# Openings of each sub-layer rebuilt around a normalised copy of x, with the order of attention, index and weight splitting changed

## The reference

```
h = rmsnorm(x, g_pre) * (1.0 + scale) + shift
x = x + resid_w * gate * rmsnorm(y_fn(h), g_post)
```

## Time and profile before

| what | value |
|---|---|
| median of 3 runs | 2760.48 us (2760.14 to 2760.69) |
| the profiled execution | 2764.69 us, span of its instructions 2761.9 us |
| TensorE busy | 2717.2 us, 98% of the span |
| VectorE busy | 1518.2 us, 55% |
| ScalarE busy | 1096.0 us, 40% |
| GpSimd busy | 269.6 us, 10% |
| granted TensorE clock, mean | 0.995 of full speed |

### The profile page before, as it was taken

How to read it: one execution, slowest core, us unless ns; L and a number is a source line. 1 busy time by engine, 2 the same in 40 slices (tenths; PEclk the granted TensorE clock), 3 DMA queues, 4 the chain that set the end, 5 groups by cost and what they waited for, 6 DMA issues and landing times.

```text
span 2761.9 us, 37653 instructions
## 1 busy us (share of the span) xinstructions
PE 2717.2 (98%) x13280; PEld 2177.1 (79%) x13280; DVE 1518.2 (55%) x2565; ACT 1096.0 (40%) x1993; POOL 269.6 (10%) x353
## 2 busy tenths in 40 slices
PE   8999999999999999999999999999999999999999
PEld 6888887676777888888888888866677778888887
DVE  6665455567746656532376553554677475553323
ACT  4322234665545343222242222446655453332221
POOL 0111000122100001110011100001221000011100
PEclk9999999999999999999999999999999999999999
DMA  8554522112222416523245545222122224152332
GB/s 301 209 203 158 160 94 86 61 54 62 70 86 75 115 54 229 182 99 107 84 157 194 197 159 153 88 77 62 54 67 70 87 75 116 68 183 91 99 107 69
DMA packets 94797, 321.85 MB, mean 117 GB/s; under 512 B 16769, under 2 KB 17153, under 8 KB 93378
## 3 DMA queue, kind: packets, MB, share of 16 engines
q1 hardware_dynamic: 94658, 320.07, 35.3%
HBM read 316.72 MB, written 2.13 MB: 115 GB/s over the span
## 4 chain that ended last, share of the span: by engine, by line
PE 87%; DVE 6%; ACT 3%; issue 2%; DVEq 1%; SPq 0%; DMA 0%; POOL 0%; ACTq 0%; POOLq 0%
PE bank L485 20%; PE bank L487 20%; PE bank L486 20%; PE bank L494 7%; PE bank L492 7%; PE bank L493 7%; PE bank L1852 2%; PE bank L1872 2%; ACT w_high L463 1%; DVE w_low L469 1%; PE bank L1843 1%; DVEq L1059 1%; PE bank L1816 1%; DVE scores_sb L1241 1%; PE bank L1738 1%
## 5 line engine op out<-in xcount | busy, mean ns | idle before, releaser
L485 PE MATMUL bank<-h_high,w_high 128*128 128x512 f32 (+1 forms) x2488 | 970.0, 390 | 13.7 <-DVE h_low L1358 11.2
L487 PE MATMUL bank<-h_high,w_low 128*128 128x512 f32 (+1 forms) x2488 | 948.7, 381 | 0.0
L486 PE MATMUL bank<-h_low,w_high 128*128 128x512 f32 (+1 forms) x2488 | 947.5, 381 | 0.0
L469 DVE TENSOR_TENSOR w_low<-w_raw,w_high 128x1024 fp32r<-128x1024 f32 x438 | 566.3, 1294 | 595.4 <-ACT w_high L463 593.8
L463 ACT ACTIVATE w_high<-w_raw 128x1024 fp32r<-128x1024 f32 x438 | 459.2, 1051 | 362.1 <-PE bank L494 319.0
L485 PEld LDWEIGHTS bank<-h_high,w_high 128*128 128x128 f32 x2488 | 472.5, 190 | 112.0 <-issue 24.5
L487 PEld LDWEIGHTS bank<-h_high,w_low 128*128 128x128 f32 x2488 | 471.0, 189 | 91.2
L486 PEld LDWEIGHTS bank<-h_low,w_high 128*128 128x128 f32 x2488 | 472.0, 190 | 84.0 <-issue 1.9
L492 PE MATMUL bank<-w_high,ffn_high 128*128 128x512 f32 x704 | 273.9, 389 | 0.0
L493 PE MATMUL bank<-w_high,ffn_low 128*128 128x512 f32 x704 | 273.9, 389 | 0.0
L494 PE MATMUL bank<-w_low,ffn_high 128*128 128x512 f32 x704 | 273.9, 389 | 0.0
(11 more groups left out here) (216 smaller groups left out, 2638.2 us busy)
## 6 DMA issues: line engine op xcount, KB each, us to landing
w_raw<-stream SPq DMA_DIRECT2D x438, 512.0 KB, 3.6
ada_raw<-ada SPq DMA_DIRECT2D x128, 512.0 KB, 3.6
ada_start<-ada SPq DMA_DIRECT2D x8, 1024.0 KB, 17.8
post_gain<-post_gain_row SPq DMA_DIRECT2D x6, 512.0 KB, 6.0
mixer_consts<-mixc SPq DMA_DIRECT2D x2, 1152.0 KB, 5.3
x<-x_in SPq DMA_DIRECT2D x4, 512.0 KB, 6.6
silu_c<-silu_row SPq DMA_DIRECT2D x4, 512.0 KB, 4.2
out<-x SPq DMA_DIRECT2D x8, 256.0 KB, 2.0
```

Of the source, the lines that this page charges most:

```text
L469: eng.tensor_tensor(wL[:, slot], raw[:, slot], wH[:, slot].bitcast(F32), ALU.subtract).then_inc(lo_ready[slot].sem, 1)
L485: eng.matmul(o, a, rhs_h, start=first, stop=False)
L486: eng.matmul(o, a, rhs_l, start=False, stop=False)
L487: return eng.matmul(o, b, rhs_h, start=False, stop=last)
```

## The change

1. x_norm: instead of building a diagonal, ACT writes x times its per-token factor into a new tile `x_norm` (in the space of h_low), one activation of 128 x 1024 for each token block; blocks 0, 1 and 2 inside the closing, block 3 in the opening. POOL's L662 goes. PE transposes x_norm plainly with the identity (`pe.transpose`, one instruction instead of two for each 128 x 128).
2. Of the 8 feature tiles of a pair, 2, 3, 6 and 7 are scaled and shifted on ACT (`full` in ACT's opening, into `h_full_act`), the others on DVE; h_high stays on ACT, h_low on DVE. A hand-written order replaces the loops.
3. DVE takes h_full of tiles 0 and 1 of the first pair, and their h_low, ahead of block 3's update of x; ACT takes block 3's squares after tiles 0 to 3.
4. Branch C's scores move from the end of every fourth step to its head.
5. `("qrope", 1)` moves from before `("wi",)` to after the eighth index step.
6. In DVE's list the `split_low` that belongs to a unit done in quarters is kept back until after the next attention step's work (or the next unit).

```diff
             yield ("att", st)
-            if st == 0:
-                yield ("scores", st)
...
-            if 0 < st < STEPS and st % 4 == 0:
-                yield ("scores", st)
...
-                ("qrope", 0), ("uq", 1), ("ukv",), ("qrope", 1), ("wi",)]
+                ("qrope", 0), ("uq", 1), ("ukv",), ("wi",)]
...
         yield ("index", n // HEADS + 1, n % HEADS)
         if n % 3 == 2:
             yield fill.pop(0)
+        if n == HEADS - 1:
+            yield ("qrope", 1)
...
+            def x_norm(l, n, tb):
+
+                s.wait_ge(rsx_ready.sem, rsx_ready.at(l, TB * n + tb + 1))
+                s.activation(xn[:, :, tb * P:(tb + 1) * P], x[:, tb].rearrange("p (k n) -> p k n", k=KD), ACT.Copy,
+                             scale=rsx[:, tb:tb + 1]).then_inc(xn_ready.sem, 1)
+
             def closing(l, n, u_last):
...
+                    if tb >= 1:
+                        x_norm(l, n, tb - 1)
                     if tb == 2:
                         split_high(s, l, u_last + 1)
...
+                    if tb < TB - 1:
+                        x_squares(l, n, tb)
...
+                high(0, 0)
+                high(0, 1)
+                full(0, 2)
+                high(0, 2)
+                full(0, 3)
+                high(0, 3)
+                x_squares(l, n, TB - 1)
+                full(0, 6)
+                high(0, 4)
+                high(0, 5)
+                x_norm(l, n, TB - 1)
+                high(0, 6)
+                full(0, 7)
+                high(0, 7)
+                split_high(s, l, u_first + LEAD)
...
-                if kind in UNIT_KINDS and it != MIXER[0] and (kind != "out" or it[1] < KD - LEAD):
+                if kind in UNIT_KINDS and kept is not None:
+                    split_low(v, l, kept)
+                    kept = None
+                if it in PARTED:
+                    kept = U_OF[it] + LEAD
+                elif kind in UNIT_KINDS and it != MIXER[0] and (kind != "out" or it[1] < KD - LEAD):
                     split_low(v, l, U_OF[it] + LEAD)
...
                     vector_attention(v, l, it[1])
+                    if kept is not None:
+
+                        split_low(v, l, kept)
+                        kept = None
...
+                mean_y(l, n, TB - 1)
+                full(0, 0)
+                full(0, 1)
+                scaled_y(TB - 1)
+                low(0, 0)
+                low(0, 1)
+                v.drain()
+                update_x(l, n, TB - 1)
+                v.drain()
+                full(0, 4)
+                low(0, 2)
+                full(0, 5)
+                low(0, 3)
+                mean_x(l, n, TB - 1)
+                for j in range(4, KD):
+                    low(0, j)
...
             def h_block(tb):
-                pe.wait_ge(diag_ready.sem, diag_ready.at(l, TB * n + tb + 1))
+                pe.wait_ge(xn_ready.sem, xn_ready.at(l, TB * n + tb + 1))
...
-                    mm = pe.matmul(bank[4 + j // 2][:, at:at + P], x[:, tb, j * P:(j + 1) * P], diag[:, tb],
-                                   start=True, stop=True)
+                    mm = pe.transpose(bank[4 + j // 2][:, at:at + P], xn[:, j, tb * P:(tb + 1) * P], ident[:, :])
...
-                if br != "C" and g % 2 == 0:
+                if br == "C" and g % 4 == 0:
+
+                    if g > 0:
+                        pe.wait_ge(shifted.sem, shifted.at(l, g))
```

More of the change, by code:

```diff
@@ L671, in closing @@
                     if not ends(l, n):
[L672 removed]
+                        rstd(l, n, tb)
             def reciprocals(l, g):
@@ L937, in opening, with full, high @@
             def opening(l, n, u_first):
[L939 to L945, removed]
+                shift = shift_col(n % NB)
+                def full(pair, j):
+                    s.wait_ge(tr_ready.sem, tr_ready.at(l, KD * (n + 1) + 4 * pair + j // 2 + 1))
+                    if j >= 6:
+                        s.wait_ge(h_ready.sem, h_ready.at(l, h_at(n) + KD * pair + j - 3))
+                    s.activation(hu_act[:, j % 2], bank[4 + j // 2][:, 2 * P * (j % 2):2 * P * (j % 2 + 1)],
+                                 ACT.Identity, scale=vecA[:, j:j + 1], bias=shift(j)).then_inc(hua_ready.sem, 1)
+                def high(pair, j):
+                    done = KD // 2 * (2 * (n + 1) + pair) + 2 * (j // 4) + j % 2 + 1
+                    if j % 4 < 2:
+                        s.wait_ge(hu_ready.sem, hu_ready.at(l, done))
+                        src = hu[:, j % 2]
+                    else:
+                        s.wait_ge(hua_ready.sem, hua_ready.at(l, done))
+                        src = hu_act[:, j % 2]
+                    s.activation(hH[:, j, 2 * P * pair:2 * P * (pair + 1)], src, ACT.Copy).then_inc(hh_ready.sem, 1)
+                high(0, 0)
[13 more added lines that the diff above has]
+                split_high(s, l, u_first + LEAD)
+                full(1, 2)
+                high(1, 0)
+                high(1, 1)
+                full(1, 3)
+                high(1, 2)
+                high(1, 3)
+                full(1, 6)
+                high(1, 4)
+                high(1, 5)
+                full(1, 7)
+                high(1, 6)
+                high(1, 7)
             def shift_col(which):
@@ L1323, in mean_x, with mean_y, scaled_y, update_x @@
                                        ).then_inc(msx_ready.sem, 1)
-            def closing(l, n, u_last):
[L1327 to L1332, removed]
+            def mean_y(l, n, tb):
+                c = slice(tb, tb + 1)
+                v.wait_ge(ssq1_ready.sem, ssq1_ready.at(l, TB * n + tb + 1))
+                v.scalar_tensor_tensor(msy[:, c], ssq1[:, c], 1.0 / D, ssq0e[:, c], ALU.mult, ALU.add
+                                       ).then_inc(msy_ready.sem, 1)
+            def scaled_y(tb):
+                v.tensor_tensor(yg1[:, :], bank[tb][:, :], gain[:, T:D], ALU.mult)
+            def update_x(l, n, tb):
+                c = slice(tb, tb + 1)
+                v.wait_ge(rsy_ready.sem, rsy_ready.at(l, TB * n + tb + 1))
+                for half, y in ((0, yg0[:, tb]), (1, yg1[:, :])):
+                    xt = x[:, tb, T * half:T * half + T]
+                    v.scalar_tensor_tensor(xt, y, rsy[:, c], xt, ALU.mult, ALU.add).then_inc(x_ready.sem, 1)
+            def closing(l, n, u_last):
+                for tb in range(TB if ends(l, n) else TB - 1):
+                    mean_y(l, n, tb)
+                    scaled_y(tb)
                     v.drain()
[L1334 to L1337, removed]
+                    update_x(l, n, tb)
                     if ends(l, n):
@@ L1352, in opening, with low @@
                 shift = shift_col(n % NB)
-                def low(i):
-                    pair, j = i // KD, i % KD
+                def low(pair, j):
                     cols = slice(2 * P * pair, 2 * P * (pair + 1))
[L1357 to L1367, removed]
+                    v.wait_ge(hh_ready.sem, hh_ready.at(l, h_at(n) + KD * pair + j + 1))
+                    v.tensor_tensor(hL[:, j, cols], (hu if j % 4 < 2 else hu_act)[:, j % 2],
+                                    hH[:, j, cols].bitcast(F32), ALU.subtract).then_inc(h_ready.sem, 1)
@@ L1376, in opening @@
+                split_low(v, l, u_first + LEAD)
+                v.drain()
+                full(1, 0)
+                full(1, 1)
+                low(1, 0)
+                low(1, 1)
+                v.drain()
+                full(1, 4)
+                low(1, 2)
+                full(1, 5)
+                for j in range(3, KD):
+                    low(1, j)
                 v.drain()
```

65 lines of the change are left out of this document (28 added, 37 removed).

## The result

The kernel after takes 2726.84 us, the median of 4 runs (2724.39 to 2729.41), beside 2760.59 (2760.14 to 2764.03) of the kernel before on the same chip: ratio 0.9875, 95% interval 0.9858 to 0.9892, which lies wholly under 1. That is 33.7 us less; the forecast had 24.3 less, and its range ended at 2727.0, 0.16 us above the measured median. The direction was right, the size too small by 9.4 us.

The account below looks back on a forecast made before the run. PE, busy for 98% of the span, was taken to bound the kernel; openings 11.0, qrope 7.3 and attention 6 sum to 24.3 us, taking the profiled 2764.7 to 2740.4, the median 4.2 lower: 2736.2 us, range 2727 to 2748.

Parts of the forecast that it names:

- I take half of the waits: 6 us: Attention, both layers: half of the 11.2 us of PE's waits taken as gain, 6 us saved.
- The bound at the good end, 14: Attention at best: all 11.2 us of waits and two half-rate stretches of 1.46 go, 14 us saved.
- The bound at the bad end: Attention at worst: 14 groups of scores wait about 1.1 us each, less 7.2 now waited at transposes: 8 lost.
- signs: Attention: waits less than half of 11.2 us, none over 0.5 at C heads; wrong if near 1 us in branch C.
- Openings: Five openings, first transpose to first 512-column product: 25.3 us each after the change, 11.0 us saved in all.
- at most 0.6: Openings: a half-rate stretch at the first products slows PE where it would idle anyway, costing at most 0.6 us.
- qrope: Index steps: moving the second rotation removes the waits for `wi` and the half-rate stretches behind them, 7.3 us saved.
- The clock falls a second time in each opening: Openings: clock falls again behind the second pair of transposes, slowing products by 7.3 us in all; 2743.5 us, chance 0.20.
- Attention gives nothing: Attention: waits only move from the transposes to the head of the scores; 18.3 us saved, 2742.2 us, chance 0.18.
- Openings give nothing: Openings: x_norm(3) delays h_block(2) by 3 us instead of 0.9, an opening takes 27.4; 2747 us, chance 0.08.
- Slower: Attention: PE stalls for `shifted` at 14 group heads and the clock falls after each, 36 us; 2778 us, chance 0.03.
- Better than all this: Both bounds at their good end, 14 us for attention and 9 for qrope; 2727 us, chance 0.04.

Follow-up runs that it names:

- e2: Kernel before with both attention edits alone: branch C's scores at the head of every fourth step and the weight splits kept back; 2750.78 us, ratio 0.9954.
- e4: Kernel before with only the weight splits kept back behind the attention step, scores where they were; 2765.3 us, ratio 1.0007.
- e5: Kernel before with only branch C's scores moved to the head of the step, weight splits as they were; 2753.85 us, ratio 0.9966.
- e9: Kernel after without the kept back split, the C scores still at the head of the step; 2734.54 us, ratio 0.9895.
- e6: Kernel after with all 32 transposes of each opening as two-instruction multiplications by the identity; 2736.28 us, ratio 0.9905.
- e1: Kernel before with only the second rotation of the queries moved behind the eighth index step; 2757.82 us, ratio 0.9979.
- e3: Kernel before with only the openings changed (points 1 to 3 of the change); 2745.46 us, ratio 0.9934.
- e10: Kernel after with two-instruction transposes in the first two blocks of each opening, plain ones in the last two; 2726.69 us, ratio 0.9866.
- e12: Kernel after with two-instruction first-pair transposes, tile 6's rounding ahead of x_norm(3) on ACT and a weight split moved forward; 2725.45 us, ratio 0.9860.

## Why the prediction was too small

**The step that failed: attention, "I take half of the waits: 6 us".** 12.6 us in the trace, 12.4 measured alone (e2). Half of the 11.2 us of listed waits is 5.6, and as a guess at idle time that was right: 5.4 less in the two layers, 4.3 of it in the list. The step was wrong to take the waits for the whole. It left nearly nothing for the two half-rate stretches behind the wait in D, about 3 us, which are gone, and nothing for the 4.2 us by which PE's busy time over the same instructions fell besides, and which are in no wait. That the bound at the good end, 14, lies so near is therefore luck: it had all 11.2 us of waits going. The bound at the bad end was wrong too: the stall at the head of the C scores is 1.0 once in each layer (L1916), where it had 1.1 fourteen times. And one wait is indeed turned into another for each edit alone (e4: all of it, e5: about half of the 12.6), but much less for the two together (e2, e9). The forecast named signs: waits under half of the 11.2, none over 0.5 at the heads of C, and as a sign of being wrong waits near 1 us there. All three went against it (6.9 left, 1.0 in each layer), and attention still gave twice the term.

**Openings: the order of the terms right, two sizes off.** 11.0 forecast, 15.7 in the traces. The sum had 25.3 for an opening: 4.65 to the first product, 8.1 to h_block(2), 12.6 for the rest. Measured without a half-rate stretch 4.24, 7.42 and 12.60, together 24.26. DVE is free at 392.3 and not at 392.6, as x_norm(1) fits into ACT's idle time but for 0.17 us (its next w_high starts at 386.59 instead of 386.42). Between the first product and h_block(2) I had waits of 0.7 and 0.9; there is 0.94 in all. So 1.0 too much in each, 5 in all, less 0.4 for the third opening, whose first wait is longer. The two stretches cost 1.1 where 0.9 was allowed for all. Five times 25.3 is also 126.5 and not 126.3. The transposes were nearly exact: 0.11 apart, 1.69 to 1.72 for a pair against 1.76, and the old ones 3.59 (e6) against 3.75, so that the second pair saves 1.9 and not 2.0. That a half-rate stretch would cost "at most 0.6" now was right (24.84), though it came in two openings and not in most.

**qrope: right in the traces.** 7.3 forecast, 7.7 in the trace of the whole, 7.2 in that of e1, whose median gives 5.4. The wait for `wi` is gone with the stretch behind it.

**Not in the sum.** 3.2 us of the traces' difference are the half-rate stretch in the mixer's first products of layer 1, of which the new openings may have a part, as said above. The profiled execution of before (2764.7) stood at the top of its runs, that of after (2724.39) at the bottom, so the medians differ by less than the traces.

**The rivals.** *The clock falls a second time in each opening*: no stretch begins behind the second pair in any opening of any trace, 0 of 40 with plain transposes there and 0 of 30 with two instructions. The rule of the Trainium skill, TensorE: Matmul & The Clock Gate, Part 4, would have had plain transposes leave the clock low; here they run 0.109 us apart at a granted clock of 1.00 and 0.213 at 0.50 (e5), so they do run at the full clock. Whether they count less for keeping it isn't settled: the 15 of 25 against 10 of 25 above leave room for that. *Attention gives nothing*: refuted by e2. *Openings give nothing*: refuted by e3; x_norm(3) delays h_block(2) by 0.9 at most and not by 3. *Slower*, PE stalling at 14 heads: e5 shows its mechanism at two groups in each layer, for 1.0 to 1.1; it needed 1.3 at all fourteen. *Better than all this* at 2727 was the nearest, but not for its reasons: it had 14 for attention by way of the waits and 9 for qrope, and the openings' 15.7 weren't in it.

**What stays open.** Why the mixer's first products, where PE waits for nothing, draw a half-rate stretch in some traces and not in others (none in after, one in each layer in e10 and e12), and in every trace with the old openings, is open. It is worth 1.6 us each time.

## What to carry to other kernels

When two edits aim at the same chain of waits, price them together: each alone was worth 0 and 8.7 us here, both together 12.4. Nor are listed waits the whole price: 4.3 us of them went, and attention got 12.6 shorter. Read idle time from the spacing of PE's starts or from its busy time over a fixed set of instructions, not from the list of waits alone. And where an engine must open a new stage, put the first two tiles of it ahead of the closing work that nobody needs yet: that one change of order was worth as much as halving the transposes.

## What was not expected of the hardware

The first pair of transposes can be twice as long at nearly no cost. Transposes of 3.73 us with a wait of 0.77 to 0.91 behind them left the clock full in 15 of 15 openings (e6, e10, e12), where 1.91 us with a wait of 2.3 to 2.7 let it fall in 15 of 25. A PE that fills its wait with work of its own can be as fast as one that waits.
